# A one-token recurrent step on TensorE: the state as weights, or as the moving operand in four column groups

## The reference, cut to what matters

```
def gdn_recurrent(S, q, k, v, g, beta):
    def step(S, xs):
        q_t, k_t, v_t, g_t, b_t = xs
        S = S * jnp.exp(g_t)[..., None, None]
        pred = jnp.einsum('bhd,bhde->bhe', k_t, S)
        S = S + jnp.einsum('bhd,bhe->bhde', k_t, (v_t - pred) * b_t[..., None])
        return S, jnp.einsum('bhd,bhde->bhe', q_t, S)
```

## Time and profile before

| | us |
|---|---|
| median of 3 runs | 1585.78 |
| lowest and highest of them | 1584.54, 1590.09 |
| the profiled execution | 1584.17 |
| its span in the trace | 1582.6 |
| TensorE busy in it | 1407.6 (89%) |
| VectorE, ScalarE, GpSimdE busy | 469.2, 242.1, 44.3 |
| block L1301, from TensorE's first matmul to the end of the last copy | 307.9 to 373.6 |

### The profile page before, as it was taken

One profiled execution on the slowest core, in us unless ns is written; L12 is line 12 of the kernel. 1 busy time (PEld: TensorE's weight loads), 2 busy tenths in 40 slices (PEclk: granted clock), 3 DMA queues, 4 the chain that ended last, 5 costly groups with the idle time before them and its releaser, 6 DMA issues.

```text
span 1582.6 us, 20598 instructions
## 1 busy us (share of the span) xinstructions
PE 1407.6 (89%) x8224; PEld 715.3 (45%) x8224; DVE 469.2 (30%) x1103; ACT 242.1 (15%) x423; POOL 44.3 (3%) x39
## 2 busy tenths in 40 slices
PE   7998499886998998999999898898898898898896
PEld 6767387753545755433333333333333333333332
DVE  1855354543221324221312212212212212212203
ACT  1143122212000244210000000000000000000002
POOL 0000000000000014000000000000000000000000
PEclk9999699866999999999999999999999999999999
DMA  8120413505516576799999999999999999999996
GB/s 347 37 81 34 176 68 134 194 1 208 221 50 234 203 245 265 293 427 424 424 428 424 424 428 424 424 428 424 424 428 424 424 428 424 424 428 424 424 428 251
DMA packets 96705, 490.64 MB, mean 310 GB/s; under 512 B 9299, under 2 KB 14511, under 8 KB 61610
## 3 DMA queue, kind: packets, MB, share of 16 engines
q1 hardware_dynamic: 94074, 468.89, 72.0%
q0 software_dynamic: 2304, 20.97, 3.4%
q10 hardware_dynamic: 280, 0.11, 0.0%
HBM read 484.00 MB, written 6.04 MB: 310 GB/s over the span
## 4 chain that ended last, share of the span: by engine, by line
PE 38%; DMA 16%; DVE 5%; issue 2%; ACT 1%; SPq 1%; POOL 1%; POOLq 0%; DVEq 0%
DMA arena<-in_w_e 16%; PE ps L1958 14%; PE ps L1994 14%; PE ps L2006 3%; PE ps L1948 1%; PE ps L1981 1%; DVE arena L2524 1%; DVE arena L2534 1%; DVE arena L2531 1%; DVE arena L2532 1%; SPq L1701 1%; DMA arena<-in_cache_mem_k 1%; PE ps L2022 1%; PE ps L2010 1%; POOL arena L2333 0%
## 5 line engine op out<-in xcount | busy, mean ns | idle before, releaser
L1958 PE MATMUL ps<-arena 128*64 128x512 f32 x2048 | 455.8, 596 | 25.4 <-DMA arena<-in_w_e 24.8
L1958 PEld LDWEIGHTS ps<-arena 128*64 128x64 f32 x2048 | 146.1, 137 | 307.1 <-issue 305.7
L1994 PE MATMUL ps<-arena 128*64 128x512 f32 x960 | 219.9, 618 | 2.7 <-ACT arena L2208 2.5
L1994 PEld LDWEIGHTS ps<-arena 128*64 128x64 f32 x960 | 78.5, 144 | 141.5 <-issue 128.7
L2531 DVE TENSOR_SCALAR arena<-ps 128x1024 f32<-128x1024 f32 x15 | 18.4, 1224 | 299.5 <-PE ps L1958 299.5
L2543 DVE COPY arena<-ps 128x512 f32<-128x512 f32 x15 | 10.4, 691 | 222.3 <-PE ps L1994 222.3
L2206 ACT ACTIVATE arena<-arena 128x1024 f32<-128x1024 f32 x15 | 15.9, 1058 | 331.4 <-DVE arena L2531 331.4
L2549 DVE TENSOR_TENSOR res<-res,ps 128x512 f32<-128x512 f32 x60 | 41.2, 687 | 81.2 <-PE ps L2006 81.2
L1981 PE MATMUL ps<-cst,arena 128*128 128x128 f32 x120 | 20.6, 328 | 43.7 <-DVE arena L2524 43.7
L1648 PE MATMUL ps<-arena 128*128 128x512 f32 x128 | 55.8, 594 | 2.3 <-DMA arena<-in_w_xv 2.3
L1941 PEld LDWEIGHTS ps<-arena 128*128 128x128 bf16 x768 | 50.3, 100 | 13.0 <-issue 12.2
(11 more groups left out here) (550 smaller groups left out, 1615.2 us busy)
## 6 DMA issues: line engine op xcount, KB each, us to landing
arena<-in_w_e SPq DMA_DIRECT2D x384, 1024.0 KB, 18.1
arena<-in_w_in SPq DMA_DIRECT2D x8, 1380.0 KB, 17.5
arena<-in_cache_mem_k SPq DMA_DIRECT2D x8, 1024.0 KB, 9.3
arena<-in_w_out SPq DMA_DIRECT2D x2, 2048.0 KB, 10.7
arena<-in_w_xk SPq DMA_DIRECT2D x1, 4096.0 KB, 20.7
arena<-in_w_xv SPq DMA_DIRECT2D x1, 4096.0 KB, 13.6
arena<-in_w_xq SPq DMA_DIRECT2D x1, 4096.0 KB, 23.1
arena<-in_cache_mem_v SPq DMA_DIRECT2D x1, 4096.0 KB, 23.2
```

The costliest lines, as they stand in the source:

```text
L1958: last = pe.matmul(ps[64 * x:64 * x + 64, c, :], xe[:, k, 64 * x:64 * x + 64], ring[n % RING][:, c * 512:(c + 1) * 512], start=False, stop ...
L1994: last = pe.matmul(ps[64 * x:64 * x + 64, 4 + c, :], aT[:, k, 64 * x:64 * x + 64], ring[(n + x) % RING][:, j * D + c * 512:j * D + (c + 1) ...
```

## The change

TensorE no longer takes the states as weights. VectorE writes q, k and v of the sample tokens into padded tiles: in `kz` and `qz` each pair of head and token has a 128 x 32 tile with a single non-zero column, the token's own, and `kpad`, `vpad` and `qkpad` hold eight tokens in 32 columns for each head. TensorE uses these as weights of 32 columns, with `tile_position=(0, 32 * h)`: head h goes to column group h and its results to the partitions 32h to 32h+31, so that one partition holds one head and token. The state is the moving operand (128 columns), and eight tokens accumulate in the same rows of PSUM. k, v and q.k are turned to the same form in the same way. All that VectorE computes is then 128 columns wide with a number for each partition (`gate_row`, `decay_row`, `qk_row`). Nothing is turned after it, and the spread delta is one instruction for all heads. For the outer products head h takes `krow` and `delta` from its 32 partitions (`tile_position=(32 * h, 0)`, 32 rows, where it was 8). The padding zeros are written by GpSimdE in the scan's block. `gate_and_squares` is moved behind attention step 27 on VectorE. TensorE waits for the padded tiles first (`padded`), and has one wait (`read`) between steps 26 and 27, where it had `delta`; the waits `turned` and `blocks` are gone.

```
@@ VectorE and ScalarE, in the first block (L794 on and L938 on)
+            nc.vector.memset(gate_row, 0.0)
...
+            for h in range(H):
+                nc.vector.tensor_copy(gate_row[32 * h:32 * h + DEC, :], gw[0:DEC, 6:8, 2 * H + h])
...
+            nc.scalar.activation(decay_row[:, 0:1], gate_row[:, 0:1], ACT.Exp)
@@ GpSimdE, in the scan's block (L1204)
+            for padded in (kz, qz):
+                nc.gpsimd.memset(padded.rearrange("p h b n -> p (h b n)"), 0.0)
+            for padded in (kpad, vpad, qkpad):
+                nc.gpsimd.memset(padded.rearrange("p h n -> p (h n)"), 0.0)
@@ VectorE, in the block L1301
-            egs = eg[:, G_SMP:G_SMP + 32].rearrange("p (h b) -> p h b", h=H)
-            bs = gsb[:, G_BSMP:G_BSMP + 32].rearrange("p (h b) -> p h b", h=H)
+            for padded, x, in ((kz, k_s), (qz, q_s)):
+                nc.vector.tensor_copy(padded.rearrange("p h b n -> p h (b n)")[:, :, 0:DEC * 32:33], x)
+            nc.vector.tensor_copy(kpad[:, :, 0:DEC], k_s)
+            nc.vector.tensor_copy(vpad[:, :, 0:DEC], v_s)
+            nc.vector.tensor_tensor(qkpad[:, :, 0:DEC], q_s, k_s, ALU.mult).then_inc(sm["padded"], 1)
             nc.vector.memset(otok[:, 2], 0.0)
-            nc.vector.tensor_tensor(pr[:, :, :], q_s, k_s, ALU.mult).then_inc(sm["prod"], 1)
-            gate_and_squares(dve, (0, 1), osq01, sig01)
+            link(nc.vector.tensor_scalar(decay_row[:, 1:2], decay_row[:, 0:1], -1.0, None, ALU.mult))
             sampled_dve(dve, STEP_HEAD)
             dve.wait_ge(sm["seen"], 1)
-            sqk = ps[:, 0, 0:64].rearrange("p (h b j) -> p h b j", h=H, j=2)
-            link(nc.vector.tensor_tensor(dT[:, :, :], sqk[:, :, :, 1], egs, ALU.mult))
-            link(nc.vector.tensor_tensor(dT[:, :, :], v_s, dT[:, :, :], ALU.subtract))
-            link(nc.vector.tensor_tensor(dT[:, :, :], dT[:, :, :], bs, ALU.mult))
-            link(nc.vector.tensor_tensor(pr[:, :, :], dT[:, :, :], ps[:, 0, 64:96].rearrange("p (h b) -> p h b", h=H), ALU.mult))
-            link(nc.vector.tensor_tensor(oT[:, :, :], sqk[:, :, :, 0], egs, ALU.mult))
-            nc.vector.tensor_tensor(oT[:, :, :], oT[:, :, :], pr[:, :, :], ALU.add).then_inc(sm["delta"], 1)
+            s_k, s_q, k_t, v_t = ps[:, 0, 0:P], ps[:, 0, P:2 * P], ps[:, 1, 0:P], ps[:, 1, P:2 * P]
+            nc.vector.tensor_copy(qk_row, ps[:, 0, 2 * P:2 * P + 1])
+            nc.vector.tensor_copy(krow, k_t)
+            link(nc.vector.tensor_copy(orow, v_t))
+            link(nc.vector.scalar_tensor_tensor(drow, s_k, decay_row[:, 1:2], orow, ALU.mult, ALU.add))
+            link(nc.vector.tensor_scalar(drow, drow, gate_row[:, 1:2], None, ALU.mult))
+            nc.vector.tensor_tensor(delta, rep1(drow, [P, DEC, P]), rep(c_(C_ROW, DEC), [P, DEC, P]), ALU.mult)
+            link(nc.vector.tensor_scalar(orow, drow, qk_row, None, ALU.mult))
+            link(nc.vector.scalar_tensor_tensor(orow, s_q, decay_row[:, 0:1], orow, ALU.mult, ALU.add))
+            for h in range(H):
+                last = nc.vector.tensor_copy(otok[0:DEC, 2, h, :], orow[32 * h:32 * h + DEC, :])
+            last.then_inc(sm["read"], 1)
             sampled_dve(dve, STEP_HEAD + 1)
-            dve.wait_ge(sm["turned"], 1)
-            nc.vector.tensor_copy(kts[:, :, :], ps[0:DEC, 1, :].rearrange("p (h n) -> p h n", h=H))
-            link(nc.vector.tensor_copy(dts[:, :, :], ps[0:DEC, 2, :].rearrange("p (h n) -> p h n", h=H)))
-            nc.vector.tensor_copy(otok[0:DEC, 2], ps[0:DEC, 3, :].rearrange("p (h n) -> p h n", h=H))
-
-            for h in range(H):
-                nc.vector.tensor_tensor(delta[:, h], rep1(dts[:, h, :], [DEC, DEC, P]), rep(c_(C_ID, DEC, DEC), [DEC, DEC, P]), ALU.mult).then_inc(sm["blocks"], 1)
+            gate_and_squares(dve, (0, 1), osq01, sig01)
+
             for h in range(H):
                 dve.wait_ge(sm["outer"], h + 1)
@@ TensorE, in the block L1301
             pe.wait_ge(state_loaded, 16)
+            pe.wait_ge(sm["padded"], 1)
+            for padded, a in ((kpad, 0), (vpad, P)):
+                for h in range(H):
+                    pe.matmul(ps[32 * h:32 * h + 32, 1, a:a + P], padded[:, h, :], ident, start=True, stop=True, tile_position=(0, 32 * h))
             for h in range(H):
+                pe.matmul(ps[32 * h:32 * h + 32, 0, 2 * P:2 * P + 1], qkpad[:, h, :], c_(C_ONE, 1), start=True, stop=True, tile_position=(0, 32 * h))
+            for padded, a in ((kz, 0), (qz, P)):
                 for b in range(DEC):
-                    a = 2 * (h * DEC + b)
-                    pe.matmul(ps[:, 0, a:a + 2], st[:, b * H + h, :], qkv[:, h:h + 5:4, SEQ + b], start=True, stop=True)
-            pe.wait_ge(sm["prod"], 1)
-            pe.matmul(ps[:, 0, 64:96], c_(C_ONE), pr[:, :, :], start=True, stop=True).then_inc(sm["seen"], 1)
+                    for h in range(H):
+                        last = pe.matmul(ps[32 * h:32 * h + 32, 0, a:a + P], padded[:, h, b, :], st[:, b * H + h, :],
+                                         start=(b == 0), stop=(b == DEC - 1), tile_position=(0, 32 * h))
+            last.then_inc(sm["seen"], 1)
             sampled_pe(pe, STEP_HEAD)
-            pe.wait_ge(sm["delta"], 1)
-            for h in range(H):
-                pe.transpose(ps[0:DEC, 1, h * P:(h + 1) * P], qkv[:, H + h, SEQ:TOK], ident)
-                pe.transpose(ps[0:DEC, 2, h * P:(h + 1) * P], dT[:, h, :], ident)
-                last = pe.transpose(ps[0:DEC, 3, h * P:(h + 1) * P], oT[:, h, :], ident)
-            last.then_inc(sm["turned"], 1)
+            pe.wait_ge(sm["read"], 1)
             sampled_pe(pe, STEP_HEAD + 1)
             for h in range(H):
-                pe.wait_ge(sm["blocks"], h + 1)
                 if h >= 2:
                     pe.wait_ge(sm["updated"], h - 1)
+                rows = slice(32 * h, 32 * h + 32)
                 for j in range(2):
-                    last = pe.matmul(ps[:, 2 * (h % 2) + j, :], kts[:, h, :], delta[:, h, 4 * j:4 * j + 4, :], start=True, stop=True)
+                    last = pe.matmul(ps[:, 2 * (h % 2) + j, :], krow[rows, :], delta[rows, 4 * j:4 * j + 4, :], start=True, stop=True, tile_position=(32 * h, 0))
                 last.then_inc(sm["outer"], 1)
```

More of the change, by code:

```diff
@@ L54 @@
 C_HEAD = C_SUB + 1
-C_ALL = C_HEAD + H
+C_ROW = C_HEAD + H
+C_ALL = C_ROW + DEC
 ARENA = 45680
@@ L93, in constants @@
     c[:, C_HEAD:C_HEAD + H] = row % 32 == np.arange(H)[None, :]
+    c[:, C_ROW:C_ROW + DEC] = row % 32 == np.arange(DEC)[None, :]
     sel = np.repeat(np.tile(np.eye(NE, dtype=np.float32), (3, 1)), SLOTS, axis=1)
@@ L297, in build @@
     gw = keepers.take([P, 8, NT * H])
-    kts, dts = keepers.take([DEC, H, P]), keepers.take([DEC, H, P])
-    dT, oT, pr = (keepers.take([P, H, DEC]) for _ in range(3))
+    krow, drow, orow = (keepers.take([P, P]) for _ in range(3))
     AT_LATENT = keepers.at
@@ L333, in build @@
     alog, dtb = (keepers.take([P, H]) for _ in range(2))
+    gate_row = keepers.take([P, 2])
+    decay_row = keepers.take([P, 2])
+    qk_row = keepers.take([P, 1])
     rk = keepers.take([P, NT, 2 * H])
@@ L415, in build @@
     Y, u, vnew, wT = decT, decT, X, CT
-    delta = Arena(arena, AT_SLOTS + 6 * 1024).take([DEC, H, DEC, P])
+    own = Arena(arena, AT_SLOTS + 6 * 1024)
+    kz, qz = (own.take([P, H, DEC, 32]) for _ in range(2))
+    kpad, vpad, qkpad = (own.take([P, H, 32]) for _ in range(3))
+    delta = own.take([P, DEC, P])
     g, beta = gw[:, 6, :].rearrange("p (t h) -> p t h", h=H), gw[:, 7, :].rearrange("p (t h) -> p t h", h=H)
@@ L1298, in gate_and_squares @@
         link(nc.vector.tensor_tensor(o, o, sig.rearrange("p t (h n) -> p (t h) n", n=P), ALU.mult))
-    sm = {n: sem("smp_" + n) for n in ("prod", "seen", "delta", "turned", "blocks", "outer", "updated")}
+    sm = {n: sem("smp_" + n) for n in ("padded", "seen", "read", "outer", "updated")}
     with nc.Block() as block:
```

## The result

The changed kernel takes 1597.47 us (median of 6 runs, 1594.02 to 1601.38) beside 1586.21 us of the kernel before on the same chip (1582.97 to 1590.09, 6 runs). The ratio is 1.0072, with a 95% interval of 1.0049 to 1.0095: slower by 11 us, where 6 us faster was forecast. The profiled execution has a span of 1596.7 us; before it was 1582.6.

What follows compares the result with a forecast made beforehand. The expert loop's weights and matmuls bound the end; an earlier block end counts fully. Start 0.6 us later, products and q.k 6.6 saved, 17.4 for 17.6 to the mark: 6.2 us off 1585.8 gives 1579.6, range 1576.0 to 1584.5.

Steps and rivals of the forecast that it cites:

- the first part: What bounds the kernel: expert loop sets the end, untouched by the change; an earlier end of block L1301 counts in full.
- groups that block each other at 215 ns a piece: Slower rival in the state products: column groups do not run side by side, 152 pieces take 32.7 us; 1604.7 us, chance 0.06.
- products and q.k: TensorE's 152 pieces at the block's start: 7.6 us where it was 14.2, ending at 316.1.
- VectorE's twelve instructions to `read`: VectorE's column instruction, PSUM copies, 128-column instructions, delta spread and last copies behind attention step 26: 4.1 us.
- TensorE's stop before step 27: TensorE, done with step 26 at 320.3, waits 2.6 us for VectorE's `read` at 322.9.
- gate and first update: VectorE behind step 27: moved gate_and_squares 4.97 us, hiding the first outer product, then the first state update 2.07 us.
- the mark against before: VectorE's copy behind the first state update, same sequence afterwards: falls at 333.5 instead of 339.71, 6.2 us earlier.
- the 5 that I took: TensorE's clock during the state products: rises 5 us after their start, between 3.0 and 7.6 us seen before.
- my two values for step 27: From `read` to the end of step 27's second copy: 2.7 us at high clock, 4.4 at low; 3.5 taken.
- that rival: Gain partly given back behind the mark: TensorE's new stops lower its clock, costing 3.0 us; 1582.6 us, chance 0.11.
- the 0.44 us that the rival took: Drains rival: each of ten group changes in products and outer products costs 0.44 us, together 4.4; 1584.0 us, chance 0.03.
- the kind clock: Case: clock rises after 3.0 us, step 27 takes 2.7, VectorE's copies 3.5; shift 8.4, 1577.4 us, chance 0.10.

Runs made afterwards that it cites:

- the address mended: The changed kernel with 56 unused columns and a shorter arena, so arena starts at a multiple of 256: 1577.41 us, ratio 0.9943; again 1576.21 us, 0.993.
- the four kernels with the late gate: The changed kernel, it with large tiles allocated first, and it twice with arena at a multiple of 256: 1597.5, 1595.5, 1577.4, 1576.2 us.
- the seven with the old step: The kernel before, and it with only a larger DRAM table or an SBUF gap moving arena: ratios 0.9998 to 1.0126 against the kernel before.

## Why the prediction was wrong

**The step that failed** is in the first part: "The change touches nothing there", of the expert loop, and with it "An earlier end of the block is thus worth its whole length, unless the clock differs later". The diff adds eight columns of constants; the costs that I added for it were those of instructions. I read the tile's growth as a matter of room and never asked what stands behind it in SBUF. The stretches of the loop would have shown the danger (DMA share 1.02 there): in a stage whose transfers are never idle the longer packets pass through, 19.6 us by the packets' sum and 18.9 in the loop here. The shift itself did pass through (the stretch between the block and the loop differs by 0.3 us, and with the address mended the time follows). None of the rivals had this mechanism; the only one on the slower side, groups that block each other at 215 ns a piece, was not what happened (42 ns).

One reading in the first part was wrong without consequence: it says that no transfer of a later stage is under way while the block runs, but in both kernels the first half of `w_out` is issued at the block's start (307.83 and 311.66) and the DMA share in after is still 0.95 from 314 to 316.

**The terms of the sum**, against the block's start at 311.66 in after (307.83 before):

| term | forecast | measured |
|---|---|---|
| start of TensorE behind the block's start | 0.6 | 0.7 |
| products and q.k | 7.6 | 6.4 |
| to the second copy of step 26 | 2.7 | 2.7 |
| VectorE's twelve instructions to `read` | 4.1 | 4.0 |
| TensorE's stop before step 27 | 2.6 | 2.6 |
| step 27 to its second copy's end | 3.5 | 2.8 |
| gate and first update | 7.0 | 7.1 |
| the mark against before | -6.2 | -8.2 |

- The products were over-priced by 1.2 us, and nearly all of it is the price of a piece. The 63 and 36 ns of the sum are the busy time of a row of 24 pieces divided by 24, and that time holds the end of the last piece (421 and 273 ns long). By the starts of the single records four pieces, one of each group, begin every 213 ns at 1.2 GHz and every 109 ns at 2.4, which is 53 and 27 ns a piece, in the new products as in the score matmuls of before. The clock rose some 4.7 us after TensorE's first matmul, near the 5 that I took: with the prices of the sum this alone would have given 7.5 us, where 6.4 were measured.
- The clock stayed high over the stop of 2.6 us (step 27 at 0.44 and 0.86 us for its groups, as in the earlier trace rows), so the low end of my two values for step 27 was right.
- The block's end: behind the mark after takes 34.0 us (335.37 to 369.36) and before 34.1 (339.71 to 373.81). Nothing is given back there, though TensorE stops for 4.20 us in step 28; that rival is out for this execution. The turn of the last softmax waits 3.06 us as before.
- Drains at a change of groups: the rows at 313.34, 327.69 and their neighbours carry no idle time, but a record overlaps the next one, and the starts tell more. At 2.4 GHz turns follow each other every 109 ns, while the first score matmul starts 201 ns after the last turn and the next turn 204 ns after the last scores (319.28 to 319.48 and 320.07 to 320.28 in after): a change costs about 0.1 us, and the same gaps stand in before. That is in line with the rule that the prediction cites, though no run isolates the cause, and it is about a quarter of the 0.44 us that the rival took. The outer products have the gap in both kernels, with 8 rows (203 ns, from 358.95) as with 32 (202 ns, from 354.43), so what the change adds is one exit behind the products.
- GpSimdE's zeros took 2.6 us where I had 2.2, and its next load came after a wait of 1.87 us for TensorE, so the cover held:

```profile
245.82 2.12 POOL L1224 MEMSET arena<- 128x1024 f32 x2 [20.62 <-SPq L1215]
247.89 0.50 POOL L1226 MEMSET arena<- 128x128 f32 x3
250.26 0.94 POOL L411 DMA_INDIRECT arena<-in_cache_latent,arena  x1 [1.87 <-PE ps L1055]
```

By its number the shift inside the block (8.2 us) is that of the kind clock (8.4), but only a part of its mechanism came true: step 27 ran at the high clock, while the rise came at 4.7 us and not at 3.0, VectorE's instructions took 4.0 us and not 3.5, and the pieces were cheaper than in any of the cases. That the two numbers meet is luck. Outside the block came a case that was not on the list. With the address mended the new step measures 10 to 11.6 us less than before; the block is on average 57.4 us in the four kernels with the late gate and 64.9 in the seven with the old step, 7.5 us. In the same executions the stretch from the block to the loop is 260.8 us in the mean with the late gate and 262.3 with the old step, 1.6 us less, and the block begins 1.1 us later; so of the gain some 2 to 4 us aren't placed.

## What to carry to other kernels

A diff has a part that no instruction shows: what it does to the addresses of everything allocated behind a tile that grows. Where the profile says that a stage's DMA engines are never idle, look up the start of the buffers that its transfers write, before and after, and keep it at a multiple of 256 bytes, by padding or by an explicit address. When a local change comes out as forecast and the total doesn't, compare the length of the stages that it doesn't touch, and then the duration of single packets: a shift of one or two per cent is easy to see there. And a price for one of many pieces is read from the distance of their starts, not from a short row's busy time divided by their number.

## What was new about the hardware

- Packets of 8,192 bytes from DRAM into SBUF took 309 ns with a destination tile that starts at a multiple of 256 bytes and 313.9 to 314.9 in the mean with one that starts 32, 64 or 128 bytes above it; packets of 4,096 bytes 159.1 to 159.3 and 163.5 to 163.7 ns. In a loop with a DMA share of 1.02 that made 947 to 949 us into 964 to 967. Offsets under 32 bytes, and reading from SBUF at such addresses, were not tried.
- Within one offset the packets fall on a few fixed durations (309, 313 and 320 ns at 32 bytes; 309, 312 and 319 at 64; 309, 312, 314 and 321 at 128). What decides between them stays open.
- A row of 128 matmul pieces with 32 weight columns and 128 moving ones, in four column groups, ran at 43 ns each (5.52 us) while the clock went from 1.2 to 2.4 GHz: 53 ns each at the low level and 27 at the high one, by their starts.
- At a change between full-array turns and column groups, or between turns and outer products of 8 or 32 rows, the starts stand some 0.1 us further apart than they otherwise do (201 to 204 ns in place of 109, at 2.4 GHz), though the rows of the timeline show no idle time.
